# Two-block transformer on one core: opening vectors by a repeated column, value projections token-major, turns, mod steps and the scan's first operands moved

## The chip, the core and the metric

The kernel runs on 1 core of one Trainium2 chip. The metric is the device time of one launch in microseconds (us). TensorE (PE) multiplies, VectorE (DVE) and ScalarE (ACT) do elementwise work, and DMA queues of SyncE (SP), ScalarE and GpSimd (POOL) bring data from HBM.

## The reference

256 tokens of width 1024 go through two blocks, all in fp32.

- First block, two layers: a SwiGLU feed-forward (width 2816), a token mixing with two kinds of attention behind one input projection, and a second feed-forward. Each sublayer's input is `rms_norm(h) * (1 + scale) + shift`, and shift, scale and gate are 1024-wide slices of `silu(c) @ ada_w + ada_b`.
- Second block, two layers on the latent stream x and a context stream: layer 0 is a gated chunk scan (retention and GLA heads) on both streams, layer 1 a window attention with context keys; each has a squared-ReLU MLP of width 4096. Modulation vectors come again from `silu(c) @ w_mod + b_mod`.

```python
mod = c_act @ ada_w[l] + ada_b[l]                   # nine vectors of 1024
n1 = modulate(rms_norm(h, norm_g[l, 0]), sh1, sc1)  # the first product needs sc1 and sh1
qa, ka, va, qd, kd, vd = jnp.split(proj, ...)       # values: va, vd
qa, ka, va, ga, qb, kb, vb, gb, lr = split_cols(h @ w_in, EVEN_SPLITS)   # scan layer, values: va, vb
kv = jnp.einsum('bhnsd,bhnse->bhnde', k_end, vc)    # contracts over tokens
```

## The kernel before

Activations are kept feature-major: 8 blocks of 128 features by 256 tokens. Every weight matrix is cut into chunks of 1 MB (2048 columns of SBUF in 128 partitions), 322 in all, in one fixed order through a ring of three slots. SP loads chunk n into `stage` when `lo_done` says that chunk n-3 is converted, ACT rounds it to `whi` (`conv`, L1332), DVE subtracts to get `wlo` (`conv`, L1803), PE multiplies: `up_chunk` (L591 to L593) makes 48 matmuls of 256 columns, with weights as stationary operand; `wide_up` and `wide_down` (L599, L600) are used in the feed-forwards and MLPs. Each engine works through a list written out by hand, and its waits on named semaphores are the only order between the engines.

**Opening.** The vectors ada(0,1) (scale) and ada(0,0) (shift) are needed before the first product. Their 8 MB come in eight quarters of 1 MB on POOL's queue (L562, `start_landed[0..7]`). In each quarter DVE accumulates one half (`first_steps`) and PE the other: `column_step` takes 8 blocks of the weights as stationary operand and a single column of silu(c) as the moving one; `column_rest` adds DVE's sums. PE meanwhile transposes x (`turn_rows(0)`), the parameter rows, and the normalised x (`turn_rows("normal")`), and issues `keep_warm` matmuls (L656), whose result nobody reads. DVE scales the rows of x by their root and then the columns (L2057, `normal_split` with `late`). SP loads chunk 0 when quarter 3 is in, chunk 1 when quarter 5 is in, chunk 2 after `column1`; POOL loads ctx and the next modulation weights after `column1` too. Before the first product, ACT makes `xhi` (L1443) and DVE `xlo` (L2062).

**Modulation vectors.** The other 36 are summed by DVE beside the products, 8 steps each (`mod_steps`, L1824 and L1827, weights by POOL L572), transposed by PE (`turn_mod`, L765), and reduced by DVE (`take_mod`, L1835). `STEPS` says how many steps DVE makes at each chunk, and `turn_at` follows from it. Step 0 of a vector waits for the turn of the vector before it in the same room.

**Mixers.** Of 9 chunks of w_in, 7 and 8 are the values vd. They are made feature-major, and then 10 transposes (L818), 2 of them for va, make them token-major, and ACT copies them.

**Scan layer** (`even("c")`, `even("x")`): 12 chunks in `EVEN_ORDER`; a norm's sum over another stream at `JOIN_AT` (PE L1070 waits for DVE's `join`); vector turns at `EVEN_TURNS`; after chunk 11 PE waits for `take_mod`, makes 16 transposes of the values and 6 keep_warms, while DVE clears six half blocks of `qd` (L2407, L2408) and computes `decays(0)`, for which PE's `intra(0)` waits. Then 8 steps u follow, in which DVE (`decays`, `scan`, `mask`), PE and ACT wait for each other.

**Window attention** (`odd`): chunk 1 of `odc` and of `odx` are values, transposed by 8 matmuls after chunk 2, copied by ACT.

Of the kernel before, what the change touches and what calls it, by code (L numbers as in the profile page):

```python
# [23 lines left out]
P = 128  # L24
T = 256
# [93 lines left out]
def program(nc, A, out_ap, book):  # L119
    ctx = ExitStack()  # L120
    with ctx:
# [102 lines left out]
        first_column = (R[:, 2, 64:72], R[:, 3, 0:8])  # L224
# [49 lines left out]
        def acc_name(m):  # L274
# [23 lines left out]
            "Mc": [0] + 3 * [1, 1, 1, 1, 2] + [1, 0, 1, 2, 0, 2, 2, 2, 0, 2, 1, 0, 1, 2, 0, 0],  # L298
# [12 lines left out]
        EVEN_TURNS = {"c": {6: even0, 10: even0 + 1}, "x": {7: even0 + 2, 10: even0 + 3}}  # L311
# [11 lines left out]
        for name, k in PHASES:  # L323
# [52 lines left out]
            "q": part(0, 8), "k": part(8, 2, 512), "v": part(12, 2, 512), "kdup": part(16, 4, 512),  # L376
            "vtok": part(24, 4), "p": [part(28 + 4 * i, 2, 512) for i in range(2)],
# [60 lines left out]
        def _(sp):  # L438
# [30 lines left out]
            def ffn(name, l, i):  # L469
                n = first[name]  # L470
                g, u, d = A["ffn_wg"][l, i], A["ffn_wu"][l, i], A["ffn_wd"][l, i]
                for j in range(PAIRS):
                    load(n + 2 * j, cols(g, j))
                    if name == "F0" and j == 0:
                        sp.wait_ge(start_landed[5], 16)
                    load(n + 2 * j + 1, cols(u, j))
                    if name == "F0" and j == 0:
                        sp.wait_ge(pe_out.sem, pe_out.at("column1"))
# [44 lines left out]
            sp.wait_ge(start_landed[3], 16)  # L523
# [32 lines left out]
        def _(pool):  # L556
# [6 lines left out]
            for m in range(NMOD):  # L563
                if m == 0:
                    pool.wait_ge(pe_out.sem, pe_out.at("column1"))
# [10 lines left out]
        def _(pe):  # L576
# [81 lines left out]
            def up_chunk(n, bank, between=None):  # L658

                pe.wait_ge(lo_done, START + n + 1)  # L660
                for f in range(2):
                    if f == 1 and between is not None:
                        between()
                    for k in range(8):
                        last = product(bank[:, f * T:f * T + T], k * 256 + f * P,
                                       (xhi[:, k, :], xlo[:, k, :]), n % RING, k == 0, k == 7)
                last.then_inc(chunk_used, 1)
# [167 lines left out]
            def column_step(i, q):  # L835
# [7 lines left out]
            def column_rest(i):  # L843

                pe.wait_ge(first_step[i], 4)
                for k in range(KB):
                    last = mm(first_column[i][:, k:k + 1], first_acc[i][:, k * P:(k + 1) * P], ones[:, 0:1],
                              start=False, stop=True, skip_group_check=True)
                last.then_inc(pe_out.sem, pe_out.next(f"column{i}"))
# [3 lines left out]
            column_step(0, 0)  # L853
            keep_warm(R[:, 0, :], 4)
            turn_rows(0)
            column_step(0, 1)
            keep_warm(R[:, 0, :], 4)
# [4 lines left out]
            for q in (2, 3):  # L862
                column_step(0, q)
                keep_warm(R[:, 0, :], 2)
            column_rest(0)
            pe.wait_ge(dve_out.sem, dve_out.at("rows"))
            pe.wait_ge(act_out.sem, act_out.at(("turned", 0)))
            turn_rows("normal")
            for q in range(4):
                column_step(1, q)  # L870
                keep_warm(R[:, 0, :], 2)
            column_rest(1)
            keep_warm(R[:, 0, :], 4)

            def mixer(l):
# [60 lines left out]
                for c in range(9):  # L936
# [7 lines left out]
                    if c:  # L944
                        up_chunk(n + c, R[:, c % 3 if c < 8 else 0, :])
# [25 lines left out]
                for t in range(2):  # L971
                    transpose(Y[:, 3, t * P:(t + 1) * P], proj[:, 5, t * P:(t + 1) * P])
                last = None
                for t, bank in enumerate((R[:, 1, :], Y[:, 2, :])):
                    for h in range(4):
                        last = transpose(bank[:, h * P:(h + 1) * P], proj[:, 14 + h, t * P:(t + 1) * P])
# [57 lines left out]
            def even(which):  # L1034
# [6 lines left out]
                for c in range(12):  # L1041
                    if c >= 3:
                        pe.wait_ge(drained.sem, drained.at(("ev", which, c - 3)))
                    if c:
# [31 lines left out]
                for g in range(4):  # L1076
                    kind, hh = g // 2, g % 2
                    for t in range(2):
# [1494 lines left out]
```

## Time and profile before

| | |
|---|---|
| median of 3 runs | 2312.75 us (2312.46 to 2312.92) |
| the profiled execution | 2312.03 us |
| its span | 2310.2 us |
| PE busy in the span | 2226.8 us, 96% |
| DVE, ACT busy | 76%, 50% |
| mean granted clock of TensorE | 0.985 |

The span is the time between the first and the last instruction; 1.8 us of the profiled execution lie outside it. A granted clock of 1.00 is 2.4 GHz, 0.50 is 1.2 GHz. PE's busy share counts matmuls of one column too, and matmuls that wait for their weights, so the clock beside it and the distance between instructions have to be read with it.

### The profile page before, as it was taken

What the parts mean: (1) busy time and instruction counts of PE and PEld (TensorE: products, weight loads), DVE (VectorE), ACT (ScalarE), POOL (GpSimd) and SP (SyncE); (2) the same over time, 40 slices, a digit from 0 to 9 for tenths busy, and PEclk for the clock granted to TensorE, in tenths of its full rate; (3) what the DMA queues carried; (4) which work ended last, traced back from release to release, by engine and by line L of the source; (5) the groups of instructions that cost most, each with busy time, mean ns of one, the idle gap of its engine ahead of it and who ended that gap; (6) DMA issues with size and microseconds to landing.
All of it is one profiled execution on the core that took longest, in us unless ns stands there. A gap on an engine that the chain in (4) does not pass through costs nothing.

```text
span 2310.2 us, 33931 instructions
## 1 busy us (share of the span) xinstructions
PE 2226.8 (96%) x14346; PEld 1951.7 (84%) x14362; DVE 1764.4 (76%) x2096; ACT 1157.7 (50%) x1445; POOL 109.5 (5%) x157
## 2 busy tenths in 40 slices
PE   8999999999999999999999889899999999999998
PEld 7888899888878889888888878778878888768886
DVE  4888787788788878778886776778778886676763
ACT  2554556555355445645534434447535734475743
POOL 1000000000000000000000000000000000000000
PEclk7999999999999999999999999999999999999999
DMA  7988665488868867548886536438868876304651
GB/s 259 317 281 307 224 225 188 146 275 278 284 219 274 309 219 237 183 146 271 276 285 213 197 114 201 147 121 283 275 214 281 295 264 207 110 19 146 208 193 55
DMA packets 330446, 505.22 MB, mean 219 GB/s; under 512 B 12327, under 2 KB 239878, under 8 KB 330295
## 3 DMA queue, kind: packets, MB, share of 16 engines
q1 hardware_dynamic: 288071, 340.70, 44.8%
q0 software_dynamic: 41616, 160.44, 20.2%
q8 instruction: 113, 1.85, 0.3%
q10 hardware_dynamic: 608, 1.92, 0.2%
q14 instruction: 38, 0.31, 0.0%
HBM read 501.98 MB, written 1.05 MB: 218 GB/s over the span
## 4 chain that ended last, share of the span: by engine, by line
PE 86%; DVE 8%; ACT 3%; issue 2%; DMA 1%; ACTq 0%; SPq 0%; DVEq 0%
PE banks L599 36%; PE banks L600 18%; PE banks L591 7%; PE banks L593 6%; PE banks L592 6%; PE banks L818 2%; DVE wlo L1803 1%; PE banks L765 1%; PE banks L656 1%; PE banks L792 1%; PE banks L840 1%; ACT whi L1332 1%; PE banks L801 1%; DMA stage<-in_ffn_wu_dram 1%; DVE arena L1827 1%
## 5 line engine op out<-in xcount | busy, mean ns | idle before, releaser
L1803 DVE TENSOR_TENSOR wlo<-stage,whi 128x2048 fp32r<-128x2048 f32 (+1 forms) x326 | 736.9, 2261 | 213.1 <-ACT whi L1332 212.3
L1332 ACT CAST whi<-stage 128x2048 fp32r<-128x2048 f32 x322 | 615.4, 1912 | 381.9 <-PE banks L600 293.5
L599 PE MATMUL banks<-xs,whi 128*128 128x512 f32 x2176 | 765.7, 397 | 8.0 <-DVE xs L2062 4.1
L600 PE MATMUL banks<-xs,wlo 128*128 128x256 f32 x2176 | 608.1, 279 | 0.0
L599 PEld LDWEIGHTS banks<-xs,whi 128*128 128x128 f32 x2176 | 408.8, 188 | 108.5 <-issue 5.8
L591 PE MATMUL banks<-xs,whi 128*128 128x256 f32 x1440 | 417.9, 290 | 11.5 <-DVE xs L1993 7.9
L600 PEld LDWEIGHTS banks<-xs,wlo 128*128 128x128 f32 x2176 | 410.8, 189 | 0.0
L592 PE MATMUL banks<-xs,whi 128*128 128x256 f32 x1440 | 409.4, 284 | 0.0
L593 PE MATMUL banks<-xs,wlo 128*128 128x256 f32 x1440 | 409.3, 284 | 0.0
L599 PE MATMUL banks<-hidden_arena,whi 128*128 128x512 f32 x992 | 354.4, 399 | 0.0
L591 PEld LDWEIGHTS banks<-xs,whi 128*128 128x128 f32 x1440 | 278.4, 193 | 21.8 <-issue 10.1
L592 PEld LDWEIGHTS banks<-xs,whi 128*128 128x128 f32 x1440 | 278.4, 193 | 1.0 <-issue 0.5
L600 PE MATMUL banks<-hidden_arena,wlo 128*128 128x256 f32 x992 | 278.8, 281 | 0.0
L593 PEld LDWEIGHTS banks<-xs,wlo 128*128 128x128 f32 x1440 | 278.2, 193 | 0.0
L1827 DVE SCALAR_TENSOR_TENSOR arena<-modw,cact,arena 128x1024 f32<-128x1024 f32 x203 | 259.9, 1280 | 7.5 <-DMA modw<-in_w_mod_dram 3.8
L599 PEld LDWEIGHTS banks<-hidden_arena,whi 128*128 128x128 f32 x992 | 186.5, 188 | 45.2
L600 PEld LDWEIGHTS banks<-hidden_arena,wlo 128*128 128x128 f32 x992 | 186.3, 188 | 0.1
L599 PE MATMUL banks<-hs,whi 128*128 128x512 f32 x336 | 122.3, 401 | 5.4 <-issue 5.4
L572 POOL DMA_DIRECT2D modw<-in_w_mod_dram x80 | 57.1, 714 | 1227.0 <-DVE arena L1827 823.9
L600 PE MATMUL banks<-hs,wlo 128*128 128x256 f32 x336 | 94.7, 282 | 0.0
L1352 ACT COPY hid<-banks 128x512 f32<-128x512 f32 x44 | 25.8, 587 | 114.1 <-PE banks L600 114.1
L572 POOL DMA_DIRECT2D modw<-in_ada_w_dram x64 | 45.7, 714 | 758.8 <-DVE arena L1827 671.7
(368 smaller groups left out, 2516.2 us busy)
## 6 DMA issues: line engine op xcount, KB each, us to landing
stage<-in_mlp_w_dram SPq DMA_DIRECT2D x96, 1024.0 KB, 5.5
modw<-in_w_mod_dram POOLq DMA_DIRECT2D x80, 1024.0 KB, 5.9
modw<-in_ada_w_dram POOLq DMA_DIRECT2D x66, 1024.0 KB, 5.6
stage<-in_ffn_wg_dram SPq DMA_DIRECT2D x44, 1024.0 KB, 5.6
stage<-in_ffn_wu_dram SPq DMA_DIRECT2D x44, 1024.0 KB, 7.5
stage<-in_ffn_wd_dram SPq DMA_DIRECT2D x44, 1024.0 KB, 7.5
stage<-in_ev_w_in_dram SPq DMA_DIRECT2D x24, 1024.0 KB, 5.5
stage<-in_w_in_dram SPq DMA_DIRECT2D x18, 1024.0 KB, 5.3
```

Of the source, the lines that this page charges most:

```text
L572: pool.dma_start(modw[:, c % 2, :].rearrange("p (a b) -> p a b", a=2), src).then_inc(mod_landed[c % 2], 16)
L591: mm(out, hi, xh, start=first_mm, stop=False, skip_group_check=True)
L592: mm(out, hi, xl, start=False, stop=False, skip_group_check=True)
L593: return mm(out, lo, xh, start=False, stop=last_mm, skip_group_check=True)
L599: mm(out, hi, pair.rearrange("p a t -> p (a t)"), start=first_mm, stop=False, skip_group_check=True)
L600: return mm(out[:, 0:T], lo, pair[:, 0, :], start=False, stop=last_mm, skip_group_check=True)
L656: mm(bank, zero.to_broadcast([P, P]), zero.to_broadcast([P, 512]), start=True, stop=True)
L818: return nc.tensor.transpose(out, src, ident[0:n, 0:n])
L1332: nc.scalar.copy(whi[:, s, :], stage[:, s, :]).then_inc(hi_done, 1)
L1352: done(nc.scalar.copy(hid[:, 2, :, :], R[:, 2:4, T:2 * T]), ("up", name, j - 1))
L1803: last = v.tensor_tensor(wlo[:, s, at], stage[:, s, at], whi[:, s, at].bitcast(F32), ALU.subtract)
L1827: v.scalar_tensor_tensor(out=acc, in0=w, scalar=cc, in1=acc, op0=ALU.mult, op1=ALU.add).then_inc(mod_step, 1)
```

## The change

- **Opening.** `column_step` becomes `row_step`: the column of silu(c), repeated 128 times by a step of 0, is the stationary operand, and the quarter's half is the moving one, two matmuls of 512 columns. The result is the vector as a row, the same in all partitions; `row_rest` adds DVE's sums with `ones` as stationary operand. DVE picks the columns out of the rows: a product with the identity, a sum, and the bias. The scaling of x's rows and columns moves from DVE to ACT. Parameters are transposed earlier, `row_step(1,0)` comes before `turn_rows("normal")`, the keep_warms between the later steps go. Chunk 0 is loaded after quarter 1, chunk 1 after quarter 3.
- **Values.** `token_chunk` takes the activations as stationary operand (128 tokens) and the weights as moving one (256 columns), 48 matmuls as before; the values come out token-major and their transposes and copies go.
- **Scan layer.** New `EVEN_ORDER` with the values at 8 to 11; first turn one chunk later (6 to 7, 7 to 8); `JOIN_AT` of x from 4 to 5; `decays(0)` and four of six clears in DVE's chunk 11, ahead of the conversion of chunk n+13; two clears at u = 2; the 6 keep_warms go.
- **Steps of Mc and M0.** The later half of `STEPS["Mc"]` is redistributed, so vector 28 is turned at chunk 17 instead of 18, and 29 at chunk 25 instead of 23. The turns of M0 stay.

```diff
-            "Mc": [0] + 3 * [1, 1, 1, 1, 2] + [1, 0, 1, 2, 0, 2, 2, 2, 0, 2, 1, 0, 1, 2, 0, 0],
+            "Mc": [0] + 3 * [1, 1, 1, 1, 2] + [1, 2, 0, 2, 2, 0, 1, 1, 0, 2, 2, 0, 1, 2, 0, 0],
-        EVEN_TURNS = {"c": {6: even0, 10: even0 + 1}, "x": {7: even0 + 2, 10: even0 + 3}}
+        EVEN_TURNS = {"c": {7: even0, 10: even0 + 1}, "x": {8: even0 + 2, 10: even0 + 3}}
-        JOIN_AT = {"c": 2, "x": 4}
+        JOIN_AT = {"c": 2, "x": 5}
-        EVEN_ORDER = (0, 1, 2, 3, 4, 5, 6, 7, 10, 11, 8, 9)
+        EVEN_ORDER = (0, 1, 6, 7, 4, 5, 10, 11, 2, 3, 8, 9)
+        EVEN_VALUES = (2, 3, 8, 9)
-            sp.wait_ge(start_landed[3], 16)
+            sp.wait_ge(start_landed[1], 16)
+            def token_chunk(n, bank):
+                pe.wait_ge(lo_done, START + n + 1)
+                for t in range(2):
+                    out = bank[:, t * T:t * T + T]
+                    for k in range(8):
+                        xh, xl = xhi[:, k, t * P:(t + 1) * P], xlo[:, k, t * P:(t + 1) * P]
+                        hi, lo = whi[:, n % RING, k * 256:k * 256 + 256], wlo[:, n % RING, k * 256:k * 256 + 256]
+                        mm(out, xh, hi, start=k == 0, stop=False, skip_group_check=True)
+                        mm(out, xh, lo, start=False, stop=False, skip_group_check=True)
+                        last = mm(out, xl, hi, start=False, stop=k == 7, skip_group_check=True)
-                for k in range(KB):
-                    mm(first_column[i][:, k:k + 1], quarter(4 * i + q)[:, 1024 + k * P:1024 + (k + 1) * P], cact[:, 0, t:t + 1],
-                       start=q == 0 and k == 0, stop=False, skip_group_check=True)
+                for h in range(2):
+                    mm(first_rows[i][:, h, :], cact[:, 0, t:t + 1].to_broadcast([P, P]), quarter(4 * i + q)[:, 1024 + h * 512:1536 + h * 512],
+                       start=q == 0, stop=False, skip_group_check=True)
...
             keep_warm(Y[:, 3, :], 12)
             pe.wait_ge(act_out.sem, act_out.at("cact"))
+            row_step(0, 0)
             keep_warm(R[:, 0, :], 4)
             turn_rows(0)
...
+            row_step(0, 1)
+            keep_warm(R[:, 0, :], 4)
+            row_step(0, 2)
+            keep_warm(R[:, 0, :], 4)
+            row_step(0, 3)
+            row_rest(0)
+            pe.wait_ge(dve_out.sem, dve_out.at("pcol"))
+            row_step(1, 0)
+            pe.wait_ge(act_out.sem, act_out.at("rows scaled"))
             turn_rows("normal")
+            for q in range(1, 4):
+                row_step(1, q)
+            row_rest(1)
...
-                link(v.tensor_tensor(mc(vec[5], 0, 8), first_column[i], pcol[:, vec[4]:vec[4] + 8], ALU.add))
+                link(v.tensor_tensor(picked, first_rows[i].rearrange("p h (k n) -> p (h k) n", k=4),
+                                     ident.unsqueeze(1).to_broadcast([P, KB, P]), ALU.mult))
+                link(v.tensor_reduce(mc(vec[5], 0, 8), picked, AX_X, ALU.add))
+                link(v.tensor_tensor(mc(vec[5], 0, 8), mc(vec[5], 0, 8), pcol[:, vec[4]:vec[4] + 8], ALU.add))
```

## Rows read from the trace of the kernel before

**Rows 1.** The page: busy times; a group of weight loads (busy, mean ns).

```profile
PE 2226.8 (96%) x14346; PEld 1951.7 (84%) x14362; DVE 1764.4 (76%) x2096; ACT 1157.7 (50%) x1445; POOL 109.5 (5%) x157
L591 PEld LDWEIGHTS banks<-xs,whi 128*128 128x128 f32 x1440 | 278.4, 193 | 21.8 <-issue 10.1
```

**Rows 2.** Waits of PE: line, releaser, us in total, times, longest.

```profile
PE banks L818 <- DVE arena L2367: 15.2, 8, 2.9
PE banks L1070 <- DVE arena L2313: 5.0, 2, 4.6
PE banks L599 <- issue: 5.4, 1, 5.4
PE banks L765 <- issue: 2.3, 1, 2.3
PE banks L599 <- DVE hid L1862: 2.1, 1, 2.1
```

**Rows 3.** Timeline of the opening: start, us, engine, line, what, idle before.

```profile
18.07 1.84 PE L840 MATMUL banks<-cact,modw 128*128 128x1 f32 x16
20.66 0.38 SPq L454 DMA_DIRECT2D stage<-in_ffn_wg_dram  x1
26.05 0.38 SPq L454 DMA_DIRECT2D stage<-in_ffn_wu_dram  x1
33.97 1.90 ACT L1332 CAST whi<-stage 128x2048 fp32r<-128x2048 f32 x1 [13.83 <-DMA stage<-in_ffn_wg_dram]
36.63 1.90 ACT L1332 CAST whi<-stage 128x2048 fp32r<-128x2048 f32 x1 [0.76 <-DMA stage<-in_ffn_wu_dram]
47.32 3.41 PE L847 MATMUL banks<-base,hid 128*128 128x1 f32 x16
51.10 3.30 ACT L1443 ACTIVATE xs<-nraw,mcol 128x256 fp32r<-128x256 f32 x8 [12.57 <-DVE ecol L2509]
52.27 0.77 PE L599 MATMUL banks<-xs,whi 128*128 128x512 f32 x1
```

**Rows 4.** Windows: PE, PEld, DVE, ACT, POOL busy, granted clock, DMA share, GB/s.

```profile
45.00:50.00 5.00, 4.76 (x23) 4.63 (x24) 0.00 (x0) 0.00 (x0) 0.00 (x0) 0.50 0.00 0
```

**Rows 5.** Chain in order of time: a matmul of 512 fp32 columns (4, recorded as 8).

```profile
1995.30 3.43 PE banks L1224 x8
```

**Rows 6.** Timeline, PE and DVE after chunk 11 of the scan layers.

```profile
1299.74 2.29 DVE L1803 TENSOR_TENSOR wlo<-stage,whi 128x2048 fp32r<-128x2048 f32 x1 [0.79 <-ACT whi L1332]
1303.22 1.96 PE L818 MATMUL banks<-base,arena 128*128 128x128 f32 x16 [1.39 <-DVE mcol L1835]
1307.53 0.85 DVE L2362 SCALAR_TENSOR_TENSOR arena<-arena 64x256 f32<-64x256 f32 x2
1309.41 0.44 PE L818 MATMUL banks<-base,arena 128*128 128x128 f32 x2 [2.92 <-DVE arena L2367]
1310.75 0.69 DVE L2374 TENSOR_TENSOR hid<-banks,base 128x512 f32<-128x512 f32 x1 [1.40 <-PE banks L1112]
1476.14 0.69 DVE L2374 TENSOR_TENSOR hid<-banks,base 128x512 f32<-128x512 f32 x1 [1.93 <-PE banks L1112]
```

**Rows 7.** Timeline around the first turn of "c", DVE, ACT and PE.

```profile
1266.00 2.28 DVE L1803 TENSOR_TENSOR wlo<-stage,whi 128x2048 fp32r<-128x2048 f32 x1
1267.31 0.59 ACT L1613 COPY arena<-banks 128x512 f32<-128x512 f32 x1 [3.37 <-PE banks L593]
1277.97 0.59 ACT L1613 COPY arena<-banks 128x512 f32<-128x512 f32 x1 [8.28 <-PE banks L593]
1283.73 0.59 ACT L1613 COPY arena<-banks 128x512 f32<-128x512 f32 x1 [3.37 <-PE banks L593]
```

**Rows 8.** Timeline of "x", DVE's `join` starts.

```profile
1418.96 1.22 DVE L2311 TENSOR_TENSOR arena<-arena 128x1024 f32<-128x1024 f32 x1
```

**Rows 9.** Timeline around Mc's chunk 24, DVE and ACT.

```profile
1698.89 1.21 DVE L1835 TENSOR_REDUCE mcol<-banks 128x8 f32<-128x1024 f32 x1
1707.71 1.91 ACT L1332 CAST whi<-stage 128x2048 fp32r<-128x2048 f32 x1 [11.55 <-PE banks L600]
```

More of the change, by code:

```diff
@@ L971, in mixer @@
                 for t in range(2):
[L972 to L976, printed above, removed]
+                    last = transpose(Y[:, 3, t * P:(t + 1) * P], proj[:, 5, t * P:(t + 1) * P])
                 last.then_inc(pe_out.sem, pe_out.next(("vtok", l)))
@@ L1075, in even @@
                 pe.wait_ge(act_out.sem, act_out.at(("la", which)))
-                for g in range(4):
-                    kind, hh = g // 2, g % 2
-                    for t in range(2):
-                        for h in range(2):
-                            f = (4 if kind == 0 else 16) + 2 * hh + h
-                            last = transpose(Y[:, g, (2 * t + h) * P:(2 * t + h + 1) * P], proj[:, f, t * P:(t + 1) * P])
-                last.then_inc(pe_out.sem, pe_out.next(("vt", which)))
-                keep_warm(R[:, 0, :], 6)
                 def head_out(u):
@@ L1480, in _ @@
             take_rows(0, resx)
+            act.wait_ge(dve_out.sem, dve_out.at("row_rs"))
+            for a in range(2):
+                last = f(xrows[:, a, :], xrows[:, a, :], ACT.Copy, scale=row_rs[:, a:a + 1])
+            done(last, "rows scaled")
+            act.wait_ge(dve_out.sem, dve_out.at("first_scale"))
+            act.wait_ge(pe_out.sem, pe_out.at(("turned", "normal")))
+            for k in range(KB):
+                last = f(nraw[:, k, :], Y[:, k // 2, (k % 2) * T:(k % 2) * T + T], ACT.Copy, scale=ec("scale", k, 1))
+            done(last, ("F0", "n"))
             conv(0)
@@ L1526, in mixer @@
                 act.wait_ge(pe_out.sem, pe_out.at(("vtok", l)))
-                nc.scalar.copy(words(part(36, 1)), Y[:, 3, 0:T])
-                for t, bank in enumerate((R[:, 1, :], Y[:, 2, :])):
-                    last = nc.scalar.copy(part(37, 2, 512)[:, t, :], bank)
-                done(last, ("vtok", l))
+                done(nc.scalar.copy(words(part(36, 1)), Y[:, 3, 0:T]), ("vtok", l))
                 def take_pt(s):
@@ L2063, in lo @@
                                                   in1=xhi[:, k, :].bitcast(F32), op0=ALU.add, op1=ALU.subtract)
-                done(normal(0), (target, "n", "first"))
-                done(normal(1), (target, "n", 0))
-                if late is not None:
-                    for q in range(1, 4):
-                        normal(2 * q)
-                        done(normal(2 * q + 1), (target, "n", q))
-                    late()
+                if not ready:
+                    done(normal(0), (target, "n", "first"))
+                    done(normal(1), (target, "n", 0))
                 dve.wait_ge(act_out.sem, act_out.at((target, "xhi", "first")))
                 lo(0).then_inc(x_split.sem, x_split.next((target, "first")))
-                if late is None:
+                if not ready:
                     normal(2)
@@ L2079, in normal_split @@
                 for q in range(1, 4):
-                    if q < 3 and late is None:
+                    if q < 3 and not ready:
                         normal(2 * q + 2)
@@ L2139, in _ @@
             dve.wait_ge(act_out.sem, act_out.at("cact"))
-            for q in range(4):
+            for q in range(3):
                 first_steps(0, q)
@@ L2143, in _ @@
             refine(row_rs, row_room, row_sum, D, 1e-6)
-            dve.wait_ge(pe_out.sem, pe_out.at(("turned", 0)))
-            for a in range(2):
-                last = v.tensor_scalar(xrows[:, a, :], xrows[:, a, :], row_rs[:, a:a + 1], None, ALU.mult)
-            done(last, "rows")
+            done(v.memset(stat[:, 61:62], 0.0), "row_rs")
             dve.wait_ge(pe_out.sem, pe_out.at("params"))
```

195 lines of the change are left out of this document (97 added, 98 removed).

## The prediction, on record before the changed kernel was seen

> **What bounds the kernel.** I read the busy times first: PE 96% of the span [rows 1], so what counts is PE's instructions and the places where PE stands still. Then the list of PE's waits: only a handful over 2 us, and nearly all lie where this change works [rows 2]. Then the timelines of those places for what is late, and windows for the granted clock, since a PE that is "busy" at 0.50 does half the work. A chunk of 48 matmuls takes 5.76 us (1277.97 to 1283.73) [rows 7]; that is the yardstick below. The first product starts at 52.27 us, while the last of the ten first transfers (eight quarters, chunks 0 and 1) was taken up at 36.63 [rows 3]: 15.6 us in which the DMA queues rest (0 GB/s at 45 to 50 us [rows 4]) and PE works through column steps at clock 0.50. The sum is made against the profiled execution, 2312.03 us (span 2310.2 plus 1.8 around it), which is 0.7 below the median 2312.75.
>
> **Opening, -10.7 us.** A `column_step` takes 1.84 us at the upper clock level and 3.41 at the lower; the clock fell between the two rows under these one-column matmuls, though PE was busy for all but 0.24 us of 45 to 50 [rows 3, 4]. A `row_step` is two matmuls of 512 fp32 columns; four took 3.43, so it costs 1.72 at the upper level [rows 5], 3.4 at the lower. So at one clock it is no cheaper; what changes is that PE streams columns all the time. Four chains run toward the first product:
> - PE: transposes of x end near 18.1, parameters near 19.1 (0.85 us of work). Behind that stand seven row steps (12.0), two rests (3.4), eight keep_warms at 0.25 (2.0) and 16 transposes (1.9 [rows 6]): 19.3 us, so `rows1` at 38.4 if the clock stays up.
> - DMA: quarter 3 landed by 20.66 and quarter 5 by 26.05, 2.7 us each [rows 3]. Chunk 0 was asked for at 20.66 and taken up at 33.97, 13.3 us for 1 MB beside POOL's quarters; asking for it 5.7 us sooner delays the quarters by some 0.5 us per quarter for two of them. Quarter 7 lands near 33.5, at worst at 36.6, when all ten are in. The last row step and rest end then at 37 to 40. By the arbitration rule of the Trainium skill (DMA: Bandwidth & Descriptors, "Queues, rings and completion order": each DMA engine alternates between the queues that have work, packet by packet) the early chunks must take bandwidth from the quarters, which speaks against moving them up; the 13.3 us agree that the slower queue gets a small share. By equal shares in bytes quarter 7 would come at 36.6 and `rows1` at 40, 1.6 later than I take.
> - ACT: columns of x scaled after the turn (31.3), 8 at 0.41 as in L1443 [rows 3], so 34.6; then chunk 0's cast (1.9) to 36.5.
> - DVE: its part of chunk 0 (2.3) to 38.8. Then the picking of the vector, which the trace before does not have: a product over 1024 from PSUM and a sum over 1024 (such a sum took 1.21 [rows 9], the product I take like the nearest two-operand row of that size, 1.22 [rows 8]; bounds 0.6, at twice the rate, and 2.4, at half), bias and gaps 0.4: 2.8. So 41.7, and from the shift to the first product 1.3, as before (51.0, just ahead of the 51.10 row, to 52.27): 43.0.
>
> That is 9.3 us earlier. PE then stands still for 4.5 us before its first product, with no keep_warm in front. Before, it entered the first chunks at 0.50 too and came up within 2.6 us; I charge 0.7 more for a longer cold start. Next, chunk 3: it landed about 16 us after `column1`, and DVE's conversion of it held `up(0)` back, for which PE waited 2.1 us [rows 2]. Chunk 2 on SP's queue and ctx and two weight loads on POOL's wait for `rows1` in the same way, so their order among each other stays and all start 12 us sooner. In the new order chunk 3's load starts 4.5 us before the first product instead of 1.5, so this wait goes. 9.3 - 0.7 + 2.1 = 10.7. Bounds: 5 if PE runs the whole opening at 0.50 (`rows1` near 43.5), 12.5 if the clock never falls.
>
> **Values, -3.0 us.** `token_chunk` has the same 48 matmuls of 256 columns; only which side is stationary changes. 14 chunks are made so. I take 0 for it: no row is nearer than the 0.12 us between matmuls with weights as stationary operand. Nothing in it is shorter, so the lower bound is 0 too; the upper is the third rival's 47 us. Removed: 8 transposes in each mixer and 8 in `odd`, at 1.96/16 = 0.12 [rows 6], 1.0 each, on the bound engine: 3.0. ACT loses copies that were hidden behind PE, worth nothing. The 0.9 us for which PE waits in each mixer for the drain of chunk 8 stays, since va still needs it.
>
> **Scan start, -9.0 us.** Before, after chunk 11 (1301.8) PE waited 1.4 for `take_mod`, transposed 16 blocks to 1305.2, and stood until 1309.41, since DVE began its clears only when the transposes were done and `decays(0)` at 1307.53 (6 clears 2.1, decays 1.9) [rows 6]. After, DVE does this in front of chunk n+13's conversion, which ran at 1299.74: take_mod 1.4 after 1298.9, four clears 1.4, decays 1.9, ready at 1303.6; conversion to 1305.9, only then `mask(0)`, which started at 1310.75. So PE's `intra(0)` comes 5.8 earlier, but DVE's chain only 4.9, and the two clears at u = 2 cost 0.7: 4.2. What is late next is DVE's conversion, in front of the mask. In "x" the mask began only at 1476.14, PE having fallen to half clock; the same sum gives 1470.6, 5.5, less 0.7: 4.8. Upper bound 10.4, if the two clears hide while DVE waits for PE; lower bound 4.5, if the 8 steps are tied to something else and keep half of it.
>
> **Turn and join, -4.4 us.** In "c" PE waited 2.3 for the last step of the vector and lost more at half clock: chunk 7 ended 10.66 after chunk 6, against 5.76 and 0.95 for the turn, 3.95 too many [rows 7]. A chunk later the vector is ready. But chunk 7 itself needs `wlo`, done at 1268.3, 1.0 after chunk 6's end [rows 7]: -3.0. In "x" PE waited 4.6 for `join` [rows 2]. DVE's join began at 1418.96 and took 2.35, so PE had ended chunk 4 at 1416.8 [rows 8]. DVE's list is not shortened: from 1418.96 on it first does one step (1.3), `la` (1.2) and a conversion (2.3), then the join, ready at 1426.1; PE ends chunk 5 at 1422.6 and waits 3.5 instead. So -1.1, with -0.3 for a shorter cold spell.
>
> **Steps of Mc, -6.7 us.** PE waited 5.4 at chunk 24 [rows 2] for vector 29 to be taken: DVE did the four residual blocks first and `take_mod` at 1698.89 [rows 9]. The wait names vectors turned before chunk 24; with 29 turned at 25, it asks only for 28. Chunk 24 also ran cold (about 1700.6 to 1707.71, 1.3 over 5.76) [rows 9]. The turn itself, 8 transposes, only moves. New wait: at chunk 17 DVE's second step is step 0 of vector 29 and needs vector 28's turn, which PE makes after chunk 17; queued behind it is the conversion of chunk 19, done 2.4 us before PE asks. M0's turns stay and it had no wait; 0.
>
> Sum: 10.7 + 3.0 + 9.0 + 4.4 + 6.7 = 33.8. 2312.0 - 33.8 = 2278.2, on the scale of the median 2279.
>
> **Rivals.**
> - *The opening stays cold or DMA-bound.* For it: a PE that waits for quarters in between; PE's clock fell there before. Against: the sum above leaves PE hardly a pause. `rows1` at 43.5 instead of 38.4, time 2284. A rule of the Trainium skill bears on the pause before the first product (TensorE: Matmul & The Clock Gate, "Why this matters for your kernels": idle gaps between bursts drop the clock); the join agrees, PE resumed at half clock after its 4.6 us. By it the first chunks and the join in "x" start cold in the new kernel as well, which I have charged.
> - *Gains handed back.* DVE's list is as long as before, so PE, sooner at each place, waits at the next conversion. For it: DVE at 76%, and it was the releaser in the scan, 15.2 us over 8 waits [rows 1, 2]. Scan 4.5 instead of 9, Mc 4 instead of 6.7, turn and join 2.5: 9 less, 2288.
> - *Token-major chunks are dearer: slower.* No row shows fp32r with activations as stationary operand. 14 x 48 = 672 matmuls start 0.12 us apart; a weight load alone took 0.19 [rows 1] and hides only because it runs ahead. If it no longer did, each would cost 0.07 more, 47 us, and the time would be 2326. It decides from 0.05 us per matmul on (34/672). Against: in both forms each matmul has its own weight load of 128 columns.
> - *Nothing at all*, 2312: only if the chain lay elsewhere; the waits in [rows 2] speak against it.
>
> **Chances.** Forecast 0.62 (2272 to 2283), cold opening 0.17, handed back 0.16, token-major dearer 0.03, nothing 0.02. The range 2270 to 2292 takes in the first three and the bounds of the opening (-12.5), the product and the scan. A change under 0.2%, 4.6 us, can't be told from none. Faster 0.95, same 0.02, slower 0.03.
>
> **What would show it.** In the profile after: first L599 matmul near 43 with granted clock 1.00 from 20 to 38 (right), or 0.50 there (cold opening). L818 down by 56 instructions and the large L1641 copy gone. PE's first scan transposes some 2 us after chunk 11, mask about 2 after that. No wait of 5 us in Mc; a wait of about 3.5 for `join` in "x". Matmuls of `token_chunk` 0.12 apart. I am wrong if PE's waits reappear under other names with the same sum, or if the picking of the vector takes more than 4 us.

## The result, and the profile after

The changed kernel takes 2280.26 us (median of 4 runs, 2279.94 to 2280.47) against 2312.76 for the kernel before on the same chip: ratio 0.9852, 95% interval 0.9837 to 0.9867. The quotient of the two medians, 0.9859, lies inside the interval. I had forecast 2279. Three executions of the experiments below took 2926 to 3611 us at a mean granted clock of 0.56 to 0.70 and are left out of their medians. The span of the profiled execution fell from 2310.2 to 2278.1, by 32.1.

To find where the 32.1 us lie I use marks: ACT casts each of the 322 chunks once, in order, so the start of the same cast in two traces tells how far one kernel is ahead there. Each column gives the kernel before minus the kernel named, in us. evc and evx are the chunks of `even("c")` and `even("x")`. Where neither a wait nor the clock differs, two traces with the same code keep their distance to 0.1 us; but a cold spell that one trace has and another has not moves a column by much more. Over the traces with the changed kernel's code in that stage, the experiments below included, the gain is 2.7 to 5.0 in c's scan and 4.4 to 6.1 in x's, and behind M0 their distance to the kernel before changes by -1.8 to 2.3.

| mark | before at | changed | opening alone | Mc alone | turns back | scan back |
|---|---|---|---|---|---|---|
| in0 (after F0) | 260.3 | 9.5 | 9.5 | -2.0 | 10.7 | 9.0 |
| F1 | 451.4 | 9.7 | 8.9 | -2.0 | 10.8 | 9.1 |
| F3 | 1037.8 | 10.3 | 9.1 | -2.1 | 11.3 | 9.6 |
| evc, chunk 3 | 1230.8 | 10.4 | 9.1 | -2.1 | 10.7 | 9.0 |
| before the scan of "c" | 1297.8 | 13.1 | 10.7 | -0.6 | 12.2 | 11.6 |
| evx, chunk 4 | 1398.5 | 18.1 | 10.1 | -0.6 | 14.9 | 13.5 |
| before the scan of "x" | 1462.7 | 20.4 | 10.5 | -0.6 | 15.1 | 15.7 |
| Mc, chunk 3 | 1555.6 | 25.5 | 11.4 | -0.6 | 21.2 | 14.7 |
| M0, chunk 3 | 1753.3 | 32.7 | 10.9 | 7.4 | 28.4 | 22.0 |
| M1, last chunk | 2271.4 | 32.4 | 10.8 | 4.9 | 29.6 | 20.2 |

The waits of PE in the changed kernel (line, releaser, us in total, times, longest):

```profile
PE banks L832 <- DVE arena L2351: 12.5, 7, 2.6
PE banks L600 <- DVE xs L2080: 8.7, 10, 4.1
...
PE banks L1083 <- DVE arena L2324: 3.7, 2, 3.3
...
PE banks L600 <- DVE hid L1869: 2.6, 1, 2.6
...
PE banks L779 <- DVE plain_hs L1838: 1.9, 1, 1.9
```

Against [rows 2]: the 5.4 in front of Mc's chunk 24 and the 2.3 of the turn are gone, the join costs 3.3 instead of 4.6, the scan's wait fell by 2.7. The 4.1 in front of the first product was hidden in slow column steps before. The wait of 2.1 that I had struck out stood behind chunk 3, for `up(0)`, and is gone; but one chunk earlier, for `gate(0)` behind chunk 2, a new one of 2.6 stands. For comparison, the old one in the kernel before:

```profile
72.04 0.68 DVE L1862 TENSOR_TENSOR hid<-hid,banks 128x512 f32<-128x512 f32 x1
72.77 0.50 PE L599 MATMUL banks<-xs,whi 128*128 128x512 f32 x1 [2.11 <-DVE hid L1862]
```

The opening, windows of the changed kernel (PE, PEld, DVE, ACT, POOL busy, granted clock, DMA share, GB/s), then its timeline:

```profile
15.00:25.00 10.00, 9.95 (x48) 5.78 (x47) 5.21 (x10) 6.46 (x9) 0.00 (x0) 1.00 1.03 404
25.00:38.00 13.00, 12.00 (x40) 5.99 (x39) 9.10 (x9) 5.76 (x10) 0.00 (x0) 1.00 0.80 293
...
43.00:48.00 5.00, 5.00 (x21) 4.30 (x21) 4.68 (x7) 1.87 (x5) 0.00 (x0) 0.66 1.04 403
```

```profile
34.93 1.98 PE L854 MATMUL banks<-plain_xs,cact 128*128 128x512 f32 x4 [1.00 <-DMA plain_xs<-in_ada_w_dram]
36.75 1.88 PE L861 MATMUL banks<-hid,base 128*128 128x512 f32 x4
38.67 1.22 DVE L2062 TENSOR_TENSOR hid<-banks,base 128x1024 f32<-128x1024 f32 x1 [0.27 <-PE banks L861]
39.93 1.22 DVE L2064 TENSOR_REDUCE mcol<-hid 128x8 f32<-128x1024 f32 x1
42.74 0.47 PE L600 MATMUL banks<-xs,whi 128*128 128x512 f32 x1 [4.11 <-DVE xs L2080]
...
38.66 0.37 SPq L455 DMA_DIRECT2D stage<-in_ffn_wg_dram  x1
...
53.34 1.91 ACT L1331 CAST whi<-stage 128x2048 fp32r<-128x2048 f32 x1 [8.48 <-DMA stage<-in_ffn_wg_dram]
55.28 2.29 DVE L1814 TENSOR_TENSOR wlo<-stage,whi 128x2048 fp32r<-128x2048 f32 x1 [7.30 <-ACT whi L1331]
...
58.23 0.50 PE L600 MATMUL banks<-xs,whi 128*128 128x512 f32 x1 [2.60 <-DVE hid L1869]
```

The last rest ends at 38.63, the picking takes 2.7 (38.67 to 41.35), the first product starts at 42.74 instead of 52.27. The clock is 1.00 through all row steps and falls to 0.50 only after the pause of 4.1 us, from 43.9 to 47.2. Chunk 2, asked for at 38.66, is taken up at 53.34: 14.7 us for 1 MB. DVE's conversion of it stands in front of the first gate, and PE waits for that until 58.23. Where the time goes is seen by queue between 43 and 51 us (packets, MB, share of the 16 DMA engines; q0 is POOL's, q1 SP's):

```profile
q0 software_dynamic: 640, 2.49, 78.1%
q1 hardware_dynamic: 701, 0.71, 25.4%
```

Both queues move about as many packets, but POOL's hold 4 KB and SP's 1 KB, so SP's queue gets little more than a fifth of the bytes.

The scan's start, in "c" and "x":

```profile
1288.71 0.85 DVE L2346 SCALAR_TENSOR_TENSOR arena<-arena 64x256 f32<-64x256 f32 x2
...
1290.45 2.28 DVE L1814 TENSOR_TENSOR wlo<-stage,whi 128x2048 fp32r<-128x2048 f32 x1
1290.68 0.41 PE L832 MATMUL banks<-base,arena 128*128 128x128 f32 x2 [1.95 <-DVE arena L2351]
1292.66 0.68 DVE L2394 TENSOR_TENSOR hid<-banks,base 128x512 f32<-128x512 f32 x1
...
1449.11 0.41 PE L832 MATMUL banks<-base,arena 128*128 128x128 f32 x2 [0.72 <-ACT arena L1629]
1450.49 0.68 DVE L2394 TENSOR_TENSOR hid<-banks,base 128x512 f32<-128x512 f32 x1
```

PE stands 1.95 us in "c" and 0.72 in "x" where it stood 2.9 behind transposes and keep_warms before [rows 6]; in "x" its first scan transposes wait only for the copy of the last chunk. The mask starts right behind the late conversion, as worked out.

### The profile page after: what moved, and what is told of

It reads as the page before. It is cut to its first block, busy times and chain, and to the rows that moved or that the text cites. A ratio compares the mean times of both kernels' runs of the same rounds, so it can differ in the third digit from the quotient of the medians.

```text
span 2278.1 us, 33536 instructions
## 1 busy us (share of the span) xinstructions
PE 2200.2 (97%) x14150; PEld 1918.3 (84%) x14162; DVE 1763.3 (77%) x2091; ACT 1155.9 (51%) x1448; POOL 109.7 (5%) x157
## 3 DMA queue, kind: packets, MB, share of 16 engines
q8 instruction: 112, 1.84, 0.3%
q10 hardware_dynamic: 608, 1.92, 0.3%
## 4 chain that ended last, share of the span: by engine, by line
PE 82%; DVE 10%; ACT 4%; DMA 2%; issue 1%; POOL 0%; ACTq 0%; DVEq 0%; POOLq 0%
PE banks L600 37%; PE banks L601 19%; PE banks L592 5%; PE banks L594 5%; PE banks L593 5%; DVE wlo L1814 2%; DMA plain_xs<-in_ada_w_dram 1%; PE banks L779 1%; PE banks L832 1%; PE banks L806 1%; ACT whi L1331 1%; PE banks L815 1%; PE banks L657 1%; DMA stage<-in_ffn_wg_dram 1%; DVE plain_hs L1838 1%
## 5 line engine op out<-in xcount | busy, mean ns | idle before, releaser
L601 PE MATMUL banks<-xs,wlo 128*128 128x256 f32 x2176 | 607.7, 279 | 0.0
L600 PEld LDWEIGHTS banks<-xs,whi 128*128 128x128 f32 x2176 | 408.9, 188 | 113.7 <-issue 10.4
L601 PEld LDWEIGHTS banks<-xs,wlo 128*128 128x128 f32 x2176 | 410.7, 189 | 0.0
L592 PE MATMUL banks<-xs,whi 128*128 128x256 f32 x1216 | 351.6, 289 | 12.7 <-DVE xs L2004 7.9
L593 PE MATMUL banks<-xs,whi 128*128 128x256 f32 x1216 | 344.6, 283 | 0.0
L594 PE MATMUL banks<-xs,wlo 128*128 128x256 f32 x1216 | 344.5, 283 | 0.0
L592 PEld LDWEIGHTS banks<-xs,whi 128*128 128x128 f32 x1216 | 233.6, 192 | 22.3 <-issue 8.8
L593 PEld LDWEIGHTS banks<-xs,whi 128*128 128x128 f32 x1216 | 233.8, 192 | 0.9 <-issue 0.5
L594 PEld LDWEIGHTS banks<-xs,wlo 128*128 128x128 f32 x1216 | 233.8, 192 | 0.0
```

What stands on the lines that cost most here:

```text
L592: mm(out, hi, xh, start=first_mm, stop=False, skip_group_check=True)
L593: mm(out, hi, xl, start=False, stop=False, skip_group_check=True)
L594: return mm(out, lo, xh, start=False, stop=last_mm, skip_group_check=True)
L600: mm(out, hi, pair.rearrange("p a t -> p (a t)"), start=first_mm, stop=False, skip_group_check=True)
L601: return mm(out[:, 0:T], lo, pair[:, 0, :], start=False, stop=last_mm, skip_group_check=True)
```

## The experiments

The 12 kernels ran in three groups of four, on three chips: parts alone and moved back; the column form and DVE's lists with everything together; the wait at 55 us. The kernel before had medians of 2315.31, 2315.25 and 2313.19 there, with single runs from 2308 to 2321; the changed kernel ran only in the comparison above. The scatter of the kernel before in the opening alone is 2 us and more (column "Mc alone": 2.0 behind the kernel before's trace at in0, with the same code up to there; its clock was at 0.50 from 21.4 to 58.9 us, in the kernel before from 24.2 to 34.5 and 37.9 to 54.9). The six traces with the changed opening lie between 8.9 and 10.7 at in0. So effects of a few us are read from marks, stage by stage, and the medians stand beside them.

**Two parts alone.** The opening in the kernel before; and, in another, one line, Mc's list of steps.

```diff
-            "Mc": [0] + 3 * [1, 1, 1, 1, 2] + [1, 0, 1, 2, 0, 2, 2, 2, 0, 2, 1, 0, 1, 2, 0, 0],
+            "Mc": [0] + 3 * [1, 1, 1, 1, 2] + [1, 2, 0, 2, 2, 0, 1, 1, 0, 2, 2, 0, 1, 2, 0, 0],
```

> The kernel before with the new opening alone: row steps, the rows picked out by VectorE, chunks 0 and 1 asked for earlier, x scaled on ScalarE. First theory (each place is worth its own term, and the opening is worth what the marks of the chunks showed in the changed kernel, 8.9 to 9.6 us): 2303.2 to 2303.9. Rival (part of the opening's gain in the changed kernel came only because later stages were shorter too, or the other way, later waits of the kernel before take some of it back): 2305 or more. By my prediction's sum, 10.7: 2302.1. In each case the wait of the second chunk pair for VectorE's conversion stands near 55 us, 2.6 us long, since the loads at 39 us are the same.

> The kernel before with one line changed, the list of steps of Mc. First theory (a wait of 5.4 at chunk 24 and the cold chunk behind it go, nothing comes back): 6.7 to 7.2 less, 2305.6 to 2306.1. Rival (handed back: PE, sooner at chunk 24, waits for the next conversion, and the gain in the changed kernel needed the other edits): 4 less or under, 2308.8 or more.

Opening alone: 2306.24 (2301.14 to 2306.70) against 2315.31, ratio 0.9951 (0.9934 to 0.9968); by marks 9.5 at in0 and 8.9 to 9.1 from F1 to "c", as in the changed kernel if its 0.6 per mixer is taken off, so it does not need the other edits. The rival's 2305 is passed only because this chip is slower: against its own 2315.31 the kernel gains 9.1. The wait near 55 us is there, with 2.1. Mc alone: 2306.23, ratio 0.9962 (0.9946 to 0.9977); by marks 8.0 in Mc (-0.6 to 7.4), more than the first theory's 7.2, so nothing is handed back there. The further 2.5 that it loses after M0 (7.4 to 4.9) I can't tie to the edit: other traces shift by 1 to 2 us in the same stages. Both kernels have the scan layers of the kernel before, and still gain 1.0 and 1.5 in "c", 1.2 and 0.0 in "x" against its trace. In "c" the reason shows: behind the wait of 2.3 at the first turn the kernel before ran at 0.50 from 1270.1 to 1273.5, and neither of these two did, which is 1.5 ahead of c's scan in both. By so much a gain that is read against that one trace is too high.

**Turn and join moved back, scan's first operands moved back**, each in the changed kernel.

```diff
-        EVEN_TURNS = {"c": {7: even0, 10: even0 + 1}, "x": {8: even0 + 2, 10: even0 + 3}}
-        JOIN_AT = {"c": 2, "x": 5}
+        EVEN_TURNS = {"c": {6: even0, 10: even0 + 1}, "x": {7: even0 + 2, 10: even0 + 3}}
+        JOIN_AT = {"c": 2, "x": 4}
```

> The changed kernel with the two turns and the join moved back (turns at 6 and 7, join at 4). First theory (the predicted terms stand: 3.0 for the turn in c, 1.4 for the join in x): 4.4 more than the changed kernel, 2284.7. Rival A (the ledger's extra of 1.2 us in x belongs to turn and join, not to the scan): 5.5 to 6 more, 2286. Rival B (the order of the chunks with values early had already made the vector ready, so that the turn at 6 costs nothing any more): under 1.5 more, 2281.5.

> The changed kernel with the scan's first clears and first operands behind the last chunk again, with six clears in front of them and the conversion ahead of them; values stay token-major, so no transposes and no large copy. First theory (the gain of 9.0 to 9.6 in the two scans is two thirds the removed transposes and only one third the moved operands): intra(0) comes some 3 us later in each scan, the mask 2.3 later, 0.7 back for the two clears, so 1.6 to 2.3 per scan, 3.2 to 4.6 in all: 2283.5 to 2284.9. Rival (the moved operands are the whole gain, the transposes lay beside DVE's work): 8 to 9 more, 2289. Rival of the other sign (the two clears inside the scan cost what the move gains): within 1 us of the changed kernel.

Turns back: 2283.71, ratio 0.9859 (0.9836 to 0.9882), an interval that overlaps the changed kernel's; the marks have to tell. The waits of 2.3 at the turn and 4.6 at the join are back:

```profile
PE banks L1083 <- DVE arena L2324: 5.0, 2, 4.6
...
PE banks L779 <- issue: 2.3, 1, 2.3
```

Over the whole stages it loses 3.4 in "c" and 1.2 in "x", 4.6 in all, where I had 4.4, but most of the 3.4 lies in the scan, whose code is the same. Ahead of the scans the edit costs 1.1 in "c" (12.2 instead of 13.1 from a start 0.2 further ahead) and 2.1 in "x" (0.2 gained there instead of 2.3), and all other traces but that of the kernel before agree with the 1.1 to 0.1. So turn and join are worth 3.2; the further 2.3 in c's scan, and 1.0 the other way in x's, lie within the scatter given above. Rival B falls; the first theory's sum is nearest, and its parts are not borne out.

Scan back: 2291.98, ratio 0.9893 (0.9875 to 0.9912). Its interval and the changed kernel's do not touch. It loses 3.1 in "c" and 6.2 in "x", 9.3 together, all of it behind the marks before the scans; by the scatter there, 6 to 9. The first theory, which gave the moved operands 3.2 to 4.6 and the removed transposes the rest, falls; the rival stands. In "x", timeline of this kernel:

```profile
1452.31 0.17 DVE L1848 TENSOR_TENSOR mcol<-mcol,pcol 128x8 f32<-128x8 f32 x1
1454.78 0.27 DVE L2418 MEMSET arena<- 64x256 f32 x1 [2.31 <-PE banks L680]
...
1456.94 0.85 DVE L2373 SCALAR_TENSOR_TENSOR arena<-arena 64x256 f32<-64x256 f32 x2
...
1458.90 0.66 PE L832 MATMUL banks<-base,arena 128*128 128x128 f32 x2 [4.31 <-DVE arena L2378]
1459.36 1.92 PE L1117 MATMUL banks<-arena,nraw 128*128 128x256 f32 x4
1461.20 1.13 PE L1130 MATMUL banks<-arena 64*64 64x128 f32 x16
```

DVE stands 2.31 us until PE has ended chunk 11, since two of the six clears are in the room of xs, which that chunk still reads. In the changed kernel only those two wait, at u = 2, and the other four and `decays(0)` run while PE multiplies. After the pause of 4.3 PE then works at 0.50: the four matmuls L1117 take 1.92 (1.03 at the upper level), until 1467; the changed kernel's cold spell there lasts from 1453.5 to 1456.9. In the two scans the changed kernel gained 5.0 + 5.1 by marks. Of these 9.2 hang on the moved operands, and 0.9 is left for the removed transposes, less than the scatter: without the early operands PE would have stood in their place.

**Is it the form of the opening or its order?** The new order with column steps again:

```diff
-                for h in range(2):
-                    mm(first_rows[i][:, h, :], cact[:, 0, t:t + 1].to_broadcast([P, P]), quarter(4 * i + q)[:, 1024 + h * 512:1536 + h * 512],
-                       start=q == 0, stop=False, skip_group_check=True)
+                for k in range(KB):
+                    mm(first_column[i][:, k:k + 1], quarter(4 * i + q)[:, 1024 + k * P:1024 + (k + 1) * P], cact[:, 0, t:t + 1],
+                       start=q == 0 and k == 0, stop=False, skip_group_check=True)
```

> The changed kernel with its new order of the opening, but the eight steps and two rests again as one-column matmuls (stationary: the weights, moving: one column of the conditioning), so nothing has to be picked out by VectorE. First theory (the form decides: one-column matmuls let the granted clock fall even in the new order): clock 0.50 in a part of 20 to 40 us, steps of 3.41 there, the last rest ends 3 to 6 us later than in the changed kernel (41.6 to 45), and the missing 2.7 us of picking give it back: first product at 41.7 to 46. Rival (the order decides: early chunks, fewer pauses, x scaled on ScalarE; the clock stays up with columns too): the last rest at 38.6, first product near 40.2, 2.6 sooner than in the changed kernel. The whole time tells little here, since PE waits for chunk 2 near 55 us: within 1.5 of the changed kernel in either case, so the place of the first product and the clock decide.

2292.11, ratio 0.9898 (0.9882 to 0.9913). Timeline of PE in it:

```profile
19.89 2.21 PE L854 MATMUL banks<-cact,arena 128*128 128x1 f32 x16
...
23.62 3.41 PE L854 MATMUL banks<-cact,arena 128*128 128x1 f32 x16
...
47.27 3.55 PE L861 MATMUL banks<-base,hid 128*128 128x1 f32 x16
52.42 0.77 PE L600 MATMUL banks<-xs,whi 128*128 128x512 f32 x1 [1.60 <-DVE xs L2075]
```

The clock falls at 21 us and stays at 0.50 to 55. PE is busy without a gap from 21 to 50.8 (29.8 us of 29.8 in the windows), but each step takes 3.41 and the last rest ends at 50.8. The first product comes at 52.42, as in the kernel before (52.27): the form carries the whole gain of the opening, the order none without it. Even my first theory's 41.7 to 46 was too mild, because it forgot that steps of 3.41 make PE, and no longer the last quarter, what ends last.

**Why PE waits at 55 us.** Four edits of the changed kernel. In the first, quarter 6 stands in a room of whi instead of chunk 2's slot, and SP asks for chunk 2 when quarter 7 is in. In the second, POOL waits for chunk 2's conversion before it loads ctx and weights. In the third, 18 keep_warms fill the pause before the first product. The fourth is the first and third together.

```diff
 # 1
-                      6: stage[:, 2, :], 7: words2(plain_xs)}
+                      6: plain_whi[:, 2, :], 7: words2(plain_xs)}
-                        sp.wait_ge(pe_out.sem, pe_out.at("rows1"))
+                        sp.wait_ge(start_landed[7], 16)
 # 2
                     pool.wait_ge(pe_out.sem, pe_out.at("rows1"))
+                    pool.wait_ge(lo_done, START + 3)
 # 3
             row_rest(1)
+            keep_warm(R[:, 3, :], 18)
```

> The changed kernel, where the quarter that stood in chunk 2's stage slot goes to a room in whi instead, so that chunk 2 is asked for when the last quarter has landed (near 35 us, when the DMA queues rest) and no longer at 38.7 beside ctx, two weight loads and the constants. First theory (the wait of 2.6 at 55 us, for VectorE's gate behind chunk 2's conversion, is a late transfer): chunk 2's cast comes before 45, the wait at 55 goes, 2.6 less than the changed kernel, 2277.7. Rival A (the wait moves on: chunk 3 or 4 is now what is late, since the same bytes still have to come): under 1 less, with a wait of 1.5 to 2.5 one or two chunks later. Rival B (the wait is VectorE's own list, not the transfer): no change.

> The changed kernel, where POOL asks for ctx and the next weights only when chunk 2 has been converted, so that chunks 2 and 3 share the DMA engines with nothing but the constants. First theory (contention: chunk 2 took 14.7 us from issue to landing because of POOL's 3 MB): chunk 2 lands by 46, the wait at 55 goes, 2.6 less, 2277.7. Rival (the late weights then hold up the steps of the first vector, and a turn in F0 or the scaling of ctx waits): a new wait of PE in F0, no gain or slower.

> The changed kernel with 18 keep_warms (matmuls of zeros) in the pause of 4.1 us before the first product. First theory: the clock stays up, the first chunks run at 1.00 instead of 0.50 for 4 us and PE comes 2 us sooner to the wait for chunk 2, which lands no sooner, so that wait grows from 2.6 to 4.6 and the time stays within 0.3 of the changed kernel. Rival (the cold start was the loss of the opening): 1.8 to 2 less, 2278.3.

> Both together: chunk 2 asked for near 35 us, and keep_warms in the pause. First theory (two losses in series, of which the late chunk hides the cold clock): 4.4 to 4.6 less than the changed kernel, 2275.8, more than the sum of what each gives alone. Rival (chunk 3 is late next): no more than 2.6 less, with PE waiting near 60 us for VectorE's work behind chunk 3 or for its conversion.

| | median | ratio to before, interval | first product | wait for the gate | ahead of the changed kernel at in0 |
|---|---|---|---|---|---|
| chunk 2 early | 2278.80 | 0.9855 (0.9840 to 0.9870) | 42.32 | none | 2.1 |
| POOL late | 2287.79 | 0.9896 (0.9881 to 0.9911) | 42.38 | see below | -4.9 |
| warm | 2283.36 | 0.9879 (0.9858 to 0.9900) | 42.46 | 3.4 | -0.8 |
| both | 2275.64 | 0.9847 (0.9832 to 0.9861) | 43.39 | none | 2.8 |

Chunk 2 early: its cast comes at 44.35 and PE goes through. First theory right: 2.1 of gain by the mark where I expected 2.6, with PE still at 0.50 from 41.1 to 47.9. Asked for later and with POOL silent, chunk 2 was cast at 46.01, 7.7 us after its issue at 38.30 instead of 14.7, so the 14.7 is contention. Two parts of it show. POOL's queue sends its first packet only some 3 to 4 us after its first request (51.04 and 55.03 in the kernel before, 38.93 and 41.71 in the changed one). Before, chunk 2 used this time alone and was in at 56.1; in the changed kernel the constants used most of it, until 41.1, and chunk 2 then had to share with POOL's larger packets. But then the weights are late (timeline of DVE in that kernel), and the conversion queued behind them makes PE wait 4.1 us and fall to 0.50:

```profile
61.34 0.75 DVE L1836 TENSOR_SCALAR arena<-modw,cact 128x1024 f32<-128x1024 f32 x1 [9.18 <-DMA modw<-in_ada_w_dram]
62.01 2.28 DVE L1815 TENSOR_TENSOR wlo<-stage,whi 128x2048 fp32r<-128x2048 f32 x1
```

Keep_warms alone: the clock stays 1.00 at the first chunks, the wait grows from 2.6 to 3.4, and the clock falls behind it instead (58.5 to 61.9). No gain, as the first theory said. With chunk 2 early as well, there is no half-speed window at all before 1200 us. That trace has its whole opening 0.65 late (chunk 0 asked for at 16.06 and not 15.41), so its 2.8 to 3.4 stand for 3.4 to 4.0, somewhat under the 4.4 that I expected, and more than 2.1 and -0.8 together.

**The lists of DVE.** First, the conversion of chunk n+13 behind the last scan step. Second, in "x", the join ahead of the conversion of chunk 7, and the last two steps of the second vector at chunk 6. Last, everything together.

```diff
 # 1
                         decays(0)
-                        conv(n + 13)
...
                 scan(7)
+                conv(n + 13)
 # 2
-            "evx": [1, 1, 0, 1, 1, 2, 0, 2, 2, 2, 0, 0],
+            "evx": [1, 1, 0, 1, 1, 2, 2, 2, 2, 0, 0, 0],
...
+                    if which == "x" and c == JOIN_AT[which]:
+                        dve.wait_ge(act_out.sem, act_out.at((other, "sq", 3)))
+                        join(other, "joined", stats_of(other)[0])
                     if c < 11:
                         conv(n + c + 2)
```

> The changed kernel with the conversion of chunk n+13 taken out from between the scan's first operands and its first mask, and put behind the last scan step. First theory (it holds the mask by 0.8 in each scan and takes 2.3 of VectorE, which bounds the scan): 0.8 to 2.3 less per scan, 1.6 to 4.6 in all. Rival (the scan is a round trip between PE, VectorE and ScalarE, and the conversion lay in a gap of it): 0 to 0.5 less. Rival of the other sign (at the end it holds up the split that PE waits for): up to 2.3 more per scan.

> The changed kernel with VectorE's list in x put in another order: the join ahead of chunk 7's conversion instead of behind it, and the last two steps of the second vector at chunk 6 (where VectorE was idle for 7.1 us) instead of chunk 9. First theory (my prediction's step for the join, VectorE's list in front of it is what PE waits for): the wait of 3.3 for the join becomes 1.0, its cold spell goes, the wait of 1.9 before the second turn goes: 2.3 + 0.7 + 1.9, 4 to 5 less, 2275.8. Rival (the weights of these steps land late, so that VectorE stands at chunk 6, and the conversion of chunk 8 behind it is late): under 2 less.

> Everything together: chunk 2 asked for near 35 us, keep_warms in the pause, the late conversion, the new list in x. If each is worth its own (3.4 to 4.4 for the opening, 1.6 for the conversions, 4 to 5 in x): 9 to 11 less than the changed kernel, 2269.5 to 2271.5. If only the opening and the list in x carry: 2272 to 2273. If gains of one are handed back by the next: 2274 or more.

Late conversion: 2279.97, ratio 0.9849 (0.9831 to 0.9867); by marks 0.1 lost in "c", and in "x" nothing that stays (0.2 ahead at evx chunk 4, 0.2 at M0 chunk 3). The rival holds: the scan is a round trip and 2.3 us of DVE's work lay in its gaps. New list in "x": 2276.64, ratio 0.9831 (0.9817 to 0.9846), by marks 3.9 gained between evx chunk 4 and M0, 4.2 of it ahead of the scan, within the 4 to 5 expected. The timelines of DVE and PE in it:

```profile
1405.76 0.69 DVE L2323 TENSOR_TENSOR arena<-arena 128x512 f32<-128x512 f32 x1
1406.49 0.42 DVE L2324 TENSOR_TENSOR arena<-arena 128x256 f32<-128x256 f32 x1
1406.83 2.28 DVE L1814 TENSOR_TENSOR wlo<-stage,whi 128x2048 fp32r<-128x2048 f32 x1
...
1406.97 0.70 PE L1083 MATMUL banks<-arena,base 128*128 128x256 f32 x2 [1.13 <-DVE arena L2324]
```

The join's wait is 1.13 and the clock stays up behind it; the wait of 1.9 before the second turn is gone. All together: 2270.53 (2268.62 to 2274.29, 5 runs), ratio to the kernel before 0.9806 (0.9790 to 0.9823), an interval that does not touch the changed kernel's 0.9837 to 0.9867. By marks 7.4 ahead of the changed kernel at M0: 3.3 to 4.1 from the opening, 4.4 in "x", nothing from the late conversion. It is faster than both kernels.

## Why the prediction was right, point by point

The sum was 33.8, measured were 32.1 (span) to 32.5 (medians). 1.5 of these are the cold spell at the first turn of "c", which the trace of the kernel before had and three others with the same order of turns had not; the four runs of the kernel before on this chip lie within 0.5 us, so it is not known how often they had it.

- **Opening, 10.7 predicted, 9.5 by marks.** (8.9 of it by chunk 8; the other 0.7 comes later in F0, where the kernels "Mc alone" and with columns gain it too.) All four chains came out: last rest 38.63 (38.4), quarter 7 at 34.9 (33.5), picking 2.7 (2.8), first product 42.74 (43.0). The step that failed is "In the new order chunk 3's load starts 4.5 us before the first product instead of 1.5, so this wait goes." It rests on the sentence that the order of the loads among each other stays. It does, but not what else they meet, and I looked only at chunk 3, not at chunk 2 in front of it. The 15.6 us in which by my first paragraph the DMA queues rest were not all empty: before, the constants (704 KB, asked for by ACT when chunk 1 is cast, at 36.6) ran in them from 37.6 to 40.4, long before chunk 2, and chunk 2 landed 5.3 us after its issue. Now ACT asks for them at 37.17, SP for chunk 2 at 38.66, POOL for ctx at 38.93 and weights at 39.64. The runs with chunk 2 early and with POOL late show that the wait is chunk 2's landing. So the 2.1 behind chunk 3 went, as I had it, and 2.6 behind chunk 2 came in its place. The cold start that I charged with 0.7 (clock 0.50 from 43.9 to 47.2, at most 1.7 of work) was hidden behind this wait, as the keep_warms alone show.
- **The rule on the clock.** The Trainium skill (TensorE: Matmul & The Clock Gate, "Why this matters for your kernels") says that idle gaps between bursts drop the clock; the trace agrees with 0.50 from 43.9 to 47.2 behind the pause of 4.1. An idle gap alone does not decide this opening: PE was busy in both forms, and the clock fell with one-column matmuls alone.
- **Values, 3.0 predicted, 1.2 by marks** (0.6 in each mixer), and the rival that token-major chunks are dearer is refuted: the matmuls at L678 to L680 start 0.12 apart. In the mixers PE's time at that place fell from 1.31 to 0.44, so the term was 0.87 and not 1.0, and a new wait of 0.25 for ACT's copies (L942) follows one chunk later. In `odd` the marks give 0.5, but traces with the same code there lie between -0.8 and 2.3, so nothing can be told of its 1.0.
- **Scan start, 9.0 predicted; 10.1 by marks (5.0 in "c", 5.1 in "x"), 7.1 to 10.1 over the traces with the same scan code, 9.3 by the run with the operands back.** The mechanism is right, the moved operands do it. The 5.0 and 5.1 differ from my 4.2 and 4.8 by less than the scatter. With the operands back DVE waits for the end of chunk 11 only in "x", and there the clock falls for longer, to 1467. Of the transposes I can show no gain of their own.
- **Turn and join, 4.4 predicted, 3.2 by the marks ahead of the scans.** The parts are off, both ways: the turn in "c" gives 1.1 and not 3.0, since 1.5 of my term was the cold spell of the one trace that I read (against that trace the gain is 2.7); the join and what follows it give 2.1 and not 1.4. The waits that I foresaw are there: 1.2 for `wlo` at chunk 7 (1.0), 3.3 for the join (3.5). One that I missed is the 1.9 before the second turn of "x", whose last step DVE makes too late since the list behind the join has moved.
- **Mc, 6.7 predicted, 7.2 in the changed kernel, 8.0 alone.** No wait over 1.9 is left between 1650 and 1990 us.
- **After `odd`** the changed kernel loses 0.9 again in M1. Other traces with the same code there shift by as much; it stays open.

The sum was close partly by luck. Opening, values and turn were 1.2, about 1.8 and 1.9 too high by the changed kernel's marks; join, scan and Mc were 0.7, 1.1 and 0.5 too low, and the 1.5 of the cold spell in the trace before was gained beside them.

## What to carry to other kernels

When a start is made shorter, list every transfer that falls into the shortened stretch, on all queues, also those whose trigger did not move: what had the DMA engines to itself before may now meet the one load that PE needs next. An operand that is prepared after a stage should be split by the room it writes: the part that touches nothing of the stage can be made while the bound engine still works, and here that was worth 9 us (6 to 9 by the scatter), where eight transposes less on the bound engine gave 0.6 in each mixer. A term that is read from one trace should be looked up in a second one with the same code, when there is a cold spell in it. Where two losses stand in series, as a cold clock and a late chunk, an edit of the first alone measures nothing; try them together before you drop one.

## What the runs showed of the hardware

- One-column fp32 matmuls with the weights as stationary operand kept PE busy in the profile, and the granted clock still fell from 1.00 to 0.50, at 21 us, and stayed there until 55. Two 512-column fp32 matmuls per step, for the same sum, kept 1.00 throughout. At the upper level a step costs the same in both forms, 1.84 and 1.7 to 1.9 us.
- 1 MB on SP's queue took 14.7 us to be taken up when 704 KB on ACT's and 3 MB on POOL's queue were asked for within 2 us of it, 7.7 with POOL silent, and 5.3 in the kernel before, where the constants were through; in the first and the last it stood 0.3 us ahead of POOL's.
- With both queues full (43 to 51 us) POOL's moved 640 packets and 2.49 MB, SP's 701 packets and 0.71 MB: nearly packet for packet, so the queue with packets of 1 KB had 22% of the bytes.
- The picking of 1024 words (product with the identity from PSUM, then the sum) cost 1.22 + 1.22 us, as much as a product of this size between operands in SBUF [rows 8].
